# Start address of the input rows of the second gate and up products: 64 instead of 192 bytes modulo 256

## What is computed

```python
hs = hs + 0.5 * swiglu(rmsnorm(hs, ffn1_norm), ffn1_w_gate, ffn1_w_up, ffn1_w_down)   # D_FF = 5632
hs = hs + token_mixing(rmsnorm(hs, mix_norm), w_in, ..., w_out)
hs = hs + 0.5 * swiglu(rmsnorm(hs, ffn2_norm), ffn2_w_gate, ffn2_w_up, ffn2_w_down)
out = rmsnorm(hs, final_norm)[:, 16:]
# swiglu(h) = (silu(h @ w_gate) * (h @ w_up)) @ w_down
```

## Time and profile before

| | |
|---|---|
| median of 3 runs | 1849.35 us (1848.39 to 1851.15) |
| the profiled execution | 1849.22 us |
| its span, first to last instruction | 1847.4 us |
| TensorE matmuls busy | 1837.3 us, 99% of the span, 14421 of them |
| VectorE, ScalarE, GpSimd busy | 1088.9, 902.8 and 5.8 us |
| granted TensorE clock, mean | 0.999 |

### The profile page before, as it was taken

The page is one execution under the profiler, slowest core; times in us unless marked ns, Lnnn a source line. Parts: engine busy times, 40 slices in busy tenths (PEclk is TensorE's granted clock), DMA queues, the critical chain, the costliest instruction groups (busy, mean ns, idle before and its releaser), DMA issues.

```text
span 1847.4 us, 34892 instructions
## 1 busy us (share of the span) xinstructions
PE 1837.3 (99%) x14421; PEld 1793.5 (97%) x14421; DVE 1088.9 (59%) x1229; ACT 902.8 (49%) x1152; POOL 5.8 (0%) x16
## 2 busy tenths in 40 slices
PE   9999999999999999999999999999999999999998
PEld 9999999999999999999999999999999999988886
DVE  7555555555554545469899887555555555544454
ACT  7443434344343444359888665444444444444443
POOL 1000000000000000000000000000000000000000
PEclk9999999999999999999999999999999999999999
DMA  7655555555567777755555566666666666656664
GB/s 234 193 174 180 173 179 177 175 181 173 180 175 179 177 177 179 180 176 175 184 184 179 174 214 190 195 194 191 192 193 194 191 193 193 216 191 190 194 188 135
DMA packets 283360, 342.29 MB, mean 185 GB/s; under 512 B 10640, under 2 KB 223986, under 8 KB 283153
## 3 DMA queue, kind: packets, MB, share of 16 engines
q1 hardware_dynamic: 282672, 340.44, 61.6%
q10 hardware_dynamic: 320, 0.53, 0.1%
q0 software_dynamic: 288, 0.19, 0.0%
HBM read 339.02 MB, written 2.10 MB: 185 GB/s over the span
## 4 chain that ended last, share of the span: by engine, by line
PE 99%; DMA 0%; ACT 0%; SPq 0%; DVE 0%; issue 0%; DVEq 0%
PE ps L526 29%; PE ps L528 29%; PE ps L527 28%; PE ps L660 4%; PE ps L661 4%; PE ps L662 4%; DMA m_rows<-in_meta_tokens 0%; PE ps L678 0%; PE ps L488 0%; PE ps L685 0%; ACT o_tok L962 0%; PE ps L557 0%; PE ps L565 0%; PE ps L564 0%; SPq L372 0%
## 5 line engine op out<-in xcount | busy, mean ns | idle before, releaser
L528 PE MATMUL ps<-x_hi,w_class__lo 128*128 128x272 f32 (+2 forms) x3200 | 901.6, 282 | 0.0
L526 PE MATMUL ps<-x_hi,w_class__hi 128*128 128x272 f32 (+2 forms) x3200 | 900.8, 281 | 0.1
L527 PE MATMUL ps<-x_lo,w_class__hi 128*128 128x272 f32 (+2 forms) x3200 | 900.3, 281 | 0.0
L977 DVE TENSOR_TENSOR w_class__lo<-raw,w_class__hi 128x1024 fp32r<-128x1024 f32 x400 | 489.2, 1224 | 421.2 <-ACT w_class__hi L744 419.8
L744 ACT ACTIVATE w_class__hi<-raw 128x1024 fp32r<-128x1024 f32 x400 | 424.3, 1061 | 563.8 <-PE ps L528 563.4
L527 PEld LDWEIGHTS ps<-x_lo,w_class__hi 128*128 128x128 f32 x3200 | 602.3, 188 | 0.0
L526 PEld LDWEIGHTS ps<-x_hi,w_class__hi 128*128 128x128 f32 x3200 | 601.6, 188 | 0.3 <-PE ps L542 0.3
L528 PEld LDWEIGHTS ps<-x_hi,w_class__lo 128*128 128x128 f32 x3200 | 601.6, 188 | 0.0
L977 DVE TENSOR_TENSOR w_same__lo<-raw,w_same__hi 128x1024 fp32r<-128x1024 f32 x200 | 244.0, 1224 | 256.9 <-ACT w_same__hi L744 256.8
L744 ACT ACTIVATE w_same__hi<-raw 128x1024 fp32r<-128x1024 f32 x200 | 211.6, 1060 | 315.5 <-PE ps L528 172.0
L528 PE MATMUL ps<-a_hi,w_same__lo 128*128 128x272 f32 x640 | 183.4, 287 | 0.0
(11 more groups left out here) (177 smaller groups left out, 1508.7 us busy)
## 6 DMA issues: line engine op xcount, KB each, us to landing
raw<-in_ffn_w_up SPq DMA_DIRECT2D x176, 512.0 KB, 3.5
raw<-in_ffn_w_down SPq DMA_DIRECT2D x176, 512.0 KB, 4.8
raw<-in_ffn_w_gate SPq DMA_DIRECT2D x175, 512.0 KB, 3.5
raw<-in_w_in SPq DMA_DIRECT2D x80, 512.0 KB, 3.6
raw<-in_w_out SPq DMA_DIRECT2D x32, 512.0 KB, 4.8
x_tok<-in_x SPq DMA_DIRECT2D x4, 512.0 KB, 7.6
gain_tok<-in_final_norm SPq DMA_DIRECT2D x1, 1024.0 KB, 4.3
out_y<-o_tok SPq DMA_DIRECT2D x2, 512.0 KB, 2.8
```

What stands on the lines that cost most here:

```text
L526: pe.matmul(dst, w_high, act_high, start=first, stop=False)
L527: pe.matmul(dst, w_high, act_low, start=False, stop=False)
L528: return pe.matmul(dst, w_low, act_high, start=False, stop=last)
L977: dve.tensor_tensor(w_lo, raw_rows(phase, s), w_hi.bitcast(F32), ALU.subtract).then_inc(lo_ready, 1)
```

## The change

The two tiles of gu2's input begin 128 bytes further in the same region. Row starts go from 192 to 64 modulo 256 (each row is 1024 bytes, so all 32 rows share the value); the weights of gu2 stay at 0. No instruction is added, removed or moved on any engine, and no semaphore, size or source changes; the tiles still end inside the region (32896 of 34816 bytes).

```diff
         x_hi = at("x_hi", x_at, [P, KD, T], F32R)
         x_lo = at("x_lo", x_at + 4 * KD * T, [P, KD, T], F32R)
-        x2_hi = at("x2_hi", x_at + 0, [P, KD, SEQ], F32R)
-        x2_lo = at("x2_lo", x_at + 0 + 4 * KD * SEQ, [P, KD, SEQ], F32R)
+        x2_hi = at("x2_hi", x_at + 128, [P, KD, SEQ], F32R)
+        x2_lo = at("x2_lo", x_at + 128 + 4 * KD * SEQ, [P, KD, SEQ], F32R)
```

## The result

The changed kernel takes 1869.02 us, median of 6 executions (1850.80 to 1869.75), against 1849.34 us for the kernel before in the same comparison (6 executions, 1848.13 to 1851.15). The ratio is 1.0083 with a 95% interval of 1.0055 to 1.0112: slower, and by the medians 19.7 us. In a second comparison four further executions gave 1867.36 to 1869.51 us, ratio 1.0100 (1.0085 to 1.0115).

The account below looks back on a forecast made before the run. TensorE's matmul pitch was taken to bound the kernel: 1849.2 us profiled, plus 0 for the writers and 0 for gu2's 4224 matmuls, gave 1849.2 us, stated as 1849.3 us by the median. The range was 1847 to 1870 us.

Parts of the forecast that it names:

- The bound: Whole kernel: TensorE ends last for 99% of the span, so only the start-to-start pitch of its matmuls reaches the end time.
- The writers: The 16 ScalarE and 16 VectorE operations between 1085.6 and 1121.9 us, costed at nothing, at most 0.4 us uncovered.
- the rival: gu2 settles in the slow pace from its first block or after its interruption: 18.2 us more, 1867.5 us, chance 0.28.
- its view of the address: gu2's address acts only while read: stages before gu2 stay alike and down2 stays at 0.227 us.
- the choice of 0 us: gu2's 4224 matmuls keep 113.4 ns each at the new row start, so 0 us is added.
- the bounds of 18.2 us either way: gu2's 4224 matmuls: a 4.3 ns step down at the low end, the slow pace throughout at the high end.
- the pair in cv is equal: In cv, 260 columns, six matmuls of c = 1 and six of c = 3, 128 bytes apart, both take 0.72 us.
- enters from out_cf at the fast pace and has kept it through its own interruption: gu2 follows out_cf's 113.3 ns and shows 276 ns per matmul before and after its interruption, supporting 0 us.
- The argument against a gain: Four places with different placements, rows at 0, 128 and 192 and 512 columns, stop at the same 113.4 ns.
- The mirrored gain: gu2's 113.4 ns hides a conflict; a 4.3 ns step down saves 18.2 us, giving 1831.1 us, chance 0.04.

## Why the prediction was wrong

**The bound held.** TensorE is busy for 99% of the span before and after, at a granted clock of 0.999 both times. The writers cost nothing (495 and 480 ns each in the slow trace), the stages before out_sc kept their pace (gu1 123.5 ns in both traces, out_sc begins at 1027.1 us in both) and so did down2 (227 ns). The loss is the pitch of 256-column matmuls. The size of the rival was right as well: 18.2 us for gu2 at the slow pace, 18.9 us measured, 19.7 us between the medians. out_sc and out_cf did differ, which the prediction named as a sign that its view of the address had failed. But several kernels here leave these two stages' instructions and addresses alone, and their traces differ there too (of 15, 9 reached the first interruption of out_sc slow), so that is the history of the execution and not the moved address.

**The step that failed** is the choice of 0 us for the 4224 matmuls of gu2, between the bounds of 18.2 us either way; measured were 18.9 us. It rested on two readings. The first was "the pair in cv is equal". I read the pieces of c = 1 and c = 3 as the price of two addresses; they are parts of one repeating pattern that runs through all four classes, and moving the weights by 64, 128 or 192 bytes leaves it at 119.2 ns. That row could not have shown an effect. A steady stream at a distance of 192 existed nowhere in the trace, and "most like the change" was not like it in the point that counts, the steadiness.

The second was that gu2 "enters from out_cf at the fast pace and has kept it through its own interruption". That the pace was the same on both sides does not mean that it was kept. Mirror cases, fast to slow and slow to fast, show that gu2's restart can end in either pace, and the kernel without the wait shows the sums alone destroying the fast pace at distance 64. So in the kernel before, the fast pace was most likely lost and regained there, which no trace shows directly. The earlier trace rows held the hint, a change of pace at a restart of the same kind, and I used it only to say that the address does not choose. The address does not choose; for gu2's restart after the sums it sets the odds, 83 of 88 against 6 of 28. And the first interruption of out_sc, slow before and after at distance 64, already said that such a restart need not end fast.

The argument against a gain had the same flaw: it took the pace of down2, with both operands at 0, for one more place that stops at 113.4 ns. gu2's rows at that distance took 120.0 ns.

**The rival that came true** was given 0.28, with the right signs to look for. Its mechanism, two streams of reads whose beat may settle after the interruption, was my supposition and is shown by no trace. With nothing changed but the starts of gu2's rows, its matmuls took 113.4, 117.4, 117.8, 118.3, 118.7 or 120.0 ns at one clock; with the rows left at 192, they took 118.7 ns over weights at 64 and 120.0 ns over weights at 192. The mirrored gain did not occur in any of the 116 executions counted above: nothing was below 1848 us.

**Three executions were not enough.** The kernel before was slow in 5 of 66 executions, which three could hardly show, and a single profile is of one execution: the first trace of the changed kernel shows gu2 as fast as before.

**What stays open.** At distance 64, a restart after gu2's sums nearly always ended fast, one at a group's start in 8 of 21, in a regular pattern, and the first of out_sc's in 7 of 15. Why was not settled, nor what makes a matmul of 256 columns take 113.4 ns in one stretch and 117.8 ns in another. That the reads of weights and rows disturb each other is argued from the effect of their distance, not shown. With the rows at 128 the times came in two sets too (near 1871 and near 1877 us), and the one trace does not say where they part.

## What to carry to other kernels

Where TensorE is the bound and streams short rows (256 to 272 columns here) while it loads weights, compare starts (start to start, over hundreds of matmuls) and not the listed durations, and look for two values of one form. If there are two, the placement modulo 256 bytes of streamed rows against loaded weights and every stop or foreign matmul in the stream are worth a test: they moved this kernel by 1 to 3%. Move both operands together, look for the best distance for each length of row, and measure the candidates in ten executions or more. A wait between two parts of such a stream should not be removed, unmeasured, on the ground that its gap is small.

## What the runs showed that I had not expected

- Removing a stall of some 0.2 us made the kernel 18 us slower (1849.6 to 1867.3 us by the medians).
- The pace is persistent: 1373 triples of matmuls in a row, 485 us, at 117.8 ns, while the same instructions run at 113.4 ns after another restart.
- The placement alone, at fixed instructions, moved the whole kernel from 1849 to 1902 us when the weights were moved in all stages, 2.9%. The best distance for 256 and 272 columns, 64, is the worst of four for 512.
- With 260 columns and rotating classes the pitch is 119.2 ns at each of the four places of the weights.
